# Reordering a decoder step: the stream's modulation slices, two places in ScalarE's list, four columns of the first stage, and unread identity products in TensorE's waits

## What is computed

```python
h = rms_norm(x, norm_mix_g) * (1 + scale1) + shift1        # modulation: silu(c) @ w_ada + b_ada, 6 x 1024 columns
q, k, v, qi, ki, wi, u, vg, g_a, g_b = split(h @ w_in)     # 512|128|128|256|64|4|512|512|1024|1024 columns
attn = sparse_attention(q, k, v, top_k(index_scores(qi, wi, ki)))   # 128 of 512 keys; samples: 256 of 2049, paged
gm = u * (tril(W_s) @ vg + b)                              # per chunk of 128
x = x + gate1 * ((g_a * attn @ w_proj_attn + g_b * gm @ w_proj_gmlp) @ w_out)
t = rms_norm(x, norm_ffn_g) * (1 + scale2) + shift2
x = x + gate2 * moe(t)                                     # best group of 4, best 2 of its 8 experts, SwiGLU width 256
```

## Time and profile before

| | |
|---|---|
| runs (3), us | median 780.42, 780.20 to 781.78 |
| the profiled execution's own time, us | 779.16 |
| its span, first to last instruction, us | 777.3 |
| TensorE busy | 733.2 us, 94% |
| VectorE busy | 409.5 us, 53% |
| ScalarE busy | 206.3 us, 27% |
| GpSimd busy | 169.5 us, 22% |
| mean granted TensorE clock, share of full | 0.988 |

### The profile page before, as it was taken

How to read it: one execution, slowest core, us unless ns; L and a number is a source line. 1 busy time by engine, 2 the same in 40 slices (tenths; PEclk the granted TensorE clock), 3 DMA queues, 4 the chain that set the end, 5 groups by cost and what they waited for, 6 DMA issues and landing times.

```text
span 777.3 us, 11077 instructions
## 1 busy us (share of the span) xinstructions
PE 733.2 (94%) x4211; PEld 454.5 (58%) x4211; DVE 409.5 (53%) x940; ACT 206.3 (27%) x418; POOL 169.5 (22%) x193
## 2 busy tenths in 40 slices
PE   5899999999999998999999999987999999999986
PEld 3444466588765565788788544555555555555442
DVE  4123299999989989820245324883532322322226
ACT  4113233414366767201200011221111111111112
POOL 2030012041000000055310002464233333333210
PEclk9999999999999999999999999997999999999999
DMA  8963032433056345553423752348999999999988
GB/s 343 407 214 104 1 108 76 185 140 119 9 197 236 133 191 218 190 174 102 152 56 150 273 220 108 110 171 349 418 428 423 427 425 426 422 426 422 425 345 329
DMA packets 29191, 187.60 MB, mean 241 GB/s; under 512 B 7194, under 2 KB 8158, under 8 KB 17742
## 3 DMA queue, kind: packets, MB, share of 16 engines
q1 hardware_dynamic: 18686, 164.86, 52.8%
q0 software_dynamic: 9536, 19.72, 7.7%
q10 hardware_dynamic: 912, 2.26, 0.8%
HBM read 180.77 MB, written 16.13 MB: 253 GB/s over the span
## 4 chain that ended last, share of the span: by engine, by line
PE 77%; DMA 11%; ACT 4%; DVE 4%; issue 2%; POOL 1%; SPq 0%; DVEq 0%; POOLq 0%; ACTq 0%
PE psum L784 22%; PE psum L1267 14%; PE psum L751 11%; PE psum L1281 7%; DMA arena<-in_experts 5%; PE psum L713 4%; PE psum L659 3%; PE psum L1260 2%; DMA ring<-in_stream 2%; ACT arena L1747 2%; PE psum L1168 1%; PE psum L971 1%; DMA arena<-in_cache_ki,stat 1%; PE psum L642 1%; PE psum L982 1%
## 5 line engine op out<-in xcount | busy, mean ns | idle before, releaser
L784 PE MATMUL psum<-hT,ring 128*128 128x260 f32 x640 | 143.2, 384 | 0.1
L784 PEld LDWEIGHTS psum<-hT,ring 128*128 128x128 f32 x640 | 120.7, 190 | 21.8 <-issue 3.3
L1747 ACT ACTIVATE arena<-psum 128x512 f32<-128x512 f32 (+11 forms) x127 | 68.5, 575 | 229.8 <-PE psum L784 70.4
L751 PE MATMUL psum<-ring,hT 128*128 128x512 f32 (+1 forms) x256 | 94.6, 523 | 0.0
L751 PEld LDWEIGHTS psum<-ring,hT 128*128 128x128 f32 x256 | 48.0, 192 | 42.8 <-issue 33.7
L1267 PE MATMUL psum<-ring,arena 128*64 128x256 f32 x608 | 70.6, 386 | 1.9 <-DMA ring<-in_experts 1.2
L1281 PE MATMUL psum<-arena 128*64 128x512 f32 x280 | 67.8, 605 | 0.8 <-issue 0.8
L1679 POOL DMA_INDIRECT expert_rows<-arena,router x34 | 34.4, 1013 | 140.2 <-DVE arena L2744 127.9
L1267 PEld LDWEIGHTS psum<-ring,arena 128*64 128x64 f32 x608 | 44.5, 140 | 32.2 <-issue 11.4
L2737 DVE COPY arena<-psum 128x128 f32<-128x128 f32 x35 | 10.2, 292 | 96.0 <-PE psum L1274 95.9
L784 PE MATMUL psum<-arena,ring 128*128 128x260 f32 x256 | 58.9, 386 | 0.0
(11 more groups left out here) (396 smaller groups left out, 945.7 us busy)
## 6 DMA issues: line engine op xcount, KB each, us to landing
ring<-in_stream SPq DMA_DIRECT2D x21, 2048.0 KB, 8.8
ring<-in_experts SPq DMA_DIRECT2D x16, 2048.0 KB, 18.7
arena<-in_experts SPq DMA_DIRECT2D x32, 1024.0 KB, 22.4
arena<-in_experts SPq DMA_DIRECT2D x11, 2048.0 KB, 23.3
hT<-in_experts SPq DMA_DIRECT2D x5, 2048.0 KB, 21.0
ring<-expert_rows SPq DMA_DIRECT2D x8, 512.0 KB, 7.4
ring<-in_stream SPq DMA_DIRECT2D x2, 1280.0 KB, 6.2
arena<-in_x_prompt SPq DMA_DIRECT2D x4, 512.0 KB, 5.7
```

Source lines behind the costliest of these rows:

```text
L751: mm = pe.matmul(psum[:, b, 0:width], hT[:, k, t * P:(t + 1) * P], w[:, k, :], start=(k == 0), stop=(k == KD - 1))
L784: mm = pe.matmul(psum[:, b0 + s, 0:HALF], w[:, k, f * P:(f + 1) * P], rhs[:, k, s * HALF:(s + 1) * HALF], start=(first and k == 0), stop=( ...
L1747: ins = act.activation(out, in_, func, scale=scale)
```

## The change

Five edits. (1) In the stream, G1 comes after ada5 and ada6 instead of before them, and ada5 takes slot 2 instead of slot 1. (2) In attention, ScalarE does the next group's exponentials before it copies the finished attention block out. (3) In routing, ScalarE's `x2T_out(1)` stands before `exponents(0)` and `square(2)`, no longer behind them. (4) The last `ada_columns(3)` stands inside `a_half(3, 0)`, after its second of four blocks. (5) A new `keep_busy(name, b, n)` puts n products of the identity matrix with itself into a bank that nothing reads; it is called at nine places (`idle0` to `idle8`) ahead of a wait.

```diff
-          + [(name, KD * 512) for name in ("G0", "ada4", "G1", "ada5", "ada6", "ada7", "ada8", "ada9", "ada10", "G2",
+          + [(name, KD * 512) for name in ("G0", "ada4", "ada5", "ada6", "G1", "ada7", "ada8", "ada9", "ada10", "G2",
                                            "G3", "ada11")]
-SLOTS = (0, 2, 1, BESIDE, 0, 2, 0, 1, 2) + (0, 1, 2, 1, 1, 0, 1, 0, 1, 0, 2, 1) + (1, 0, 2, 1)
+SLOTS = (0, 2, 1, BESIDE, 0, 2, 0, 1, 2) + (0, 1, 2, 1, 2, 0, 1, 0, 1, 0, 2, 1) + (1, 0, 2, 1)
...
-            def a_half(t, h):
+            def a_half(t, h, after={}):
...
+                    if k in after:
+                        after[k]()
...
+            def keep_busy(name, b, n):
+
+                banks.begin(pe, name, b)
+                for i in range(n):
+                    mm = pe.matmul(psum[:, b, 0:P], ident, ident, start=True, stop=True)
+                    if i == 0:
+                        banks.filled(mm, name)
+                banks.drained(mm, name)
+
             pe.wait_ge(const_in, 16)
+            keep_busy("idle0", 3, 16)
             x_transposes_of(0)
...
             x_transposes_of(1)
+            keep_busy("idle8", 3, 3)
             x_transposes_of(2)
+            keep_busy("idle1", 3, 3)
             x_transposes_of(3)
...
             ada_product(2, 1)
+            keep_busy("idle2", 0, 2)
             ada_columns(2)
+            keep_busy("idle3", 0, 4)
             ring_wait(pe, "A")
...
-            a_half(3, 0)
-            ada_columns(3)
+            a_half(3, 0, {1: lambda: ada_columns(3)})
...
                 banks.filled(mm, ("qkiT", t))
+                if t == 1:
+                    keep_busy("idle4", 2, 3)
...
                          "counts")
+            keep_busy("idle5", 4, 3)
             pick_sums(4)
+            keep_busy("idle6", 4, 2)
...
             gate_sums(4)
+            keep_busy("idle7", 6, 7)
...
                     evac(("probsT", g, c), [(probsT[:, c, :], psum[:, 4 + c % 2, :])])
+                if g + 1 < N_GROUPS:
+                    exponentials(g + 1)
                 if jp == 1:
                     evac(("att", qb), [(attT[:, :, qb * P:(qb + 1) * P],
                                         psum[:, 6 + qb % 2, :].rearrange("p (j n) -> p j n", j=4))])
-                if g + 1 < N_GROUPS:
-                    exponentials(g + 1)
...
             t2_store(0)
+            x2T_out(1)
             exponents(0)
             square(2)
-            x2T_out(1)
             t2_store(1)
```

## The result

| kernel | median us | lowest to highest | executions |
|---|---|---|---|
| before | 781.1 | 780.2 to 784.2 | 4 |
| changed | 772.04 | 770.36 to 775.75 | 4 |

The medians differ by 9.1 us, against 10.5 predicted. The ratio is 0.9889, with a 95% interval of 0.9856 to 0.9922. It is an estimate of its own, and here and in the experiments it differs by up to 0.002 from the quotient of the two medians, so a difference of 1 to 2 us between ratios says nothing. The profiled execution took 770.36 us with a span of 768.6 (before 777.3) and a mean clock of 0.993.

A forecast was written before the change was run, and what follows sets the result against it. TensorE's chain was taken to bound the time before the first gather, the weights' stream the expert stage after. Terms 0.9+1.4+1.0+1.4+2.4+2.6+1.0-0.2 = 10.5 us give 769.9 from 780.42; own range 767.5 to 772, 8-in-10 766.5 to 774.5.

The forecast's parts named there:

- rival B: Attention: VectorE sets the pace, ScalarE's reordering gives 1.0 and the DMA waits' 2.4 comes by half; 772.7 us, chance 0.12.
- The stream, 2.4: Attention: TensorE's DMA waits for ada5 and ada6, 1.12 and 1.28 us, go; 2.4 us gained.
- ScalarE in attention, 2.6: Attention: exponentials first remove 0.6 of TensorE's 1.04 us wait and all of the 2.04; 2.6 us gained.
- Routing, 1.0: Routing: TensorE's 1.66 us wait for ScalarE's copy goes, VectorE is late next, so 1.0 us goes on.
- Rival C: Routing gives nothing because VectorE and GpSimd fall into another pattern; 770.9 us, chance 0.1.
- `idle6`, -0.2: Ahead of `tables`: its products exceed the 0.51 us wait and `tables` writes the same bank; 0.2 us lost.
- `ada_columns(3)`, 1.0: First stage: moved columns let VectorE start modulating sooner, removing TensorE's 1.01 us wait before 48.87; 1.0 us gained.
- The clock: 0.9 + 1.4 + 1.4: First stage: identity products give 0.9 us at the start and prevent falls near 28 and 76 us, 1.4 each.
- Rival A: First stage: the clock falls all the same at 28 or 76 us, or first products stay slow; 773.6, chance 0.2.
- What bounds the expert stage: Expert stage: the weights' stream bounds it, its amount fixed from 531.51 us, so the end moves with that point.
- The late clock, 0: First expert block: a held clock makes products 1.6 us faster, but the weights' stream hides it; 0 gained.
- Rivals D and E: Expert stage: new interleaving slows the weights' stream (slower, 0.03); or its start is fixed by something else (780.4, 0.03).

The follow-up runs named there:

- routing_only: Kernel before with only ScalarE's `x2T_out(1)` moved ahead of `exponents(0)` in routing: 782.09 us, ratio 1.001.
- stream_act: Kernel before with the stream's new order and ScalarE's exponentials ahead of the attention block's copy, together: 777.4 us, ratio 0.9929.
- no_late_idle: Changed kernel without `idle5`, `idle6` and `idle7`: 774.31 us, ratio 0.9884.
- idle_only: Kernel before with the nine `keep_busy` calls and nothing else of the change: 781.59 us, ratio 0.9982.
- idle_transposes: Changed kernel with each identity product replaced by two transposes of the identity: 772.64 us, ratio 0.9868.
- half_down: Changed kernel loading only the first half of each down matrix for 26 late-stream experts: 767.35 us, ratio 0.9812.
- no_start_idle: Changed kernel without `idle0`, `idle8` and `idle1`: 772.19 us, ratio 0.9863.
- group 1: The first four experiments (no_idle, idle_only, stream_only, act_only), run on one chip beside the kernel before, which took 783.74 us there.
- stream_only: Kernel before with only the new order and slots of the stream: 782.35 us, ratio 0.9977.
- act_only: Kernel before with only ScalarE's exponentials ahead of the attention block's copy: 778.79 us, ratio 0.9931.
- changed again: The changed kernel, unedited, measured a second time beside the kernel before: 773.49 us, ratio 0.9898.
- no_idle: Changed kernel without any of the nine `keep_busy` calls, its four reorderings kept: 774.84 us, ratio 0.9889.

## Why the prediction was right, and where it was not

The time, 772.04, lies in the 8-in-10 range (766.5 to 774.5), 2.1 us above the point and at the very edge of the forecast's own range (to 772), near rival B's 772.7. The mechanisms of attention and routing were right. The clock's terms were right in size and wrong in that they were expected each time. The first stage gives 2.35 us in the mean over the traces, for 4.7 predicted, and this shortfall is as large as the whole miss. Term by term:

- **The stream, 2.4.** Both DMA waits went, 2.55 us at their place in every kernel with the edit. But its net worth in attention is 1.44: alone it loses 1.11, 0.98 of waits for VectorE among it, and the loss is not an accident of that run, since the pair gives 4.79 where the two alone would give 5.91. This is the half of rival B that came true.
- **ScalarE in attention, 2.6.** 3.35 for itself, 2.2 behind the stream's edit, because 0.34 of the 1.04 is then left, and VectorE holds TensorE up by 0.32 at 248.40. The prediction had this remainder (0.4), but charged it to the ScalarE edit alone. Sum of both terms: 5.0 predicted, 4.79 measured, 4.77 in the changed kernel.
- **Routing, 1.0.** 1.17 to 1.22 in that stretch in nine of nine traces. Rival C fell there; the median of routing_only does not show the gain.
- **`idle6`, -0.2.** 0.3 at full clock, about 0.5 at half.
- **`ada_columns(3)`, 1.0.** 1.17: the second column is 26.30 with the identity products and 25.13 with the edit beside them, both without a fall in it; it is 26.31 in stream_act, with neither and without a fall in it.
- **Price of an identity product, 0.27 and 0.49.** Four took 1.14 in the changed kernel at full clock, 2.05 in no_late_idle at half: 0.28 and 0.51. The 16 of `idle0` took 5.54 for an estimated 6.
- **The clock: 0.9 + 1.4 + 1.4.** These sizes are right when they come. A fall at 28 costs 1.71, one at 76 1.6. In the changed kernel's profiled execution none came, and the stage gave 4.66 for 4.7 predicted. That match was luck. The step that failed is "the fall at 28 should not come", and with it the 0.9 of `idle0`. With these products in the code the clock fell between 20 and 35 us in four of six traces (idle_only, idle_transposes, no_late_idle, half_down), 3.4 to 13.7 us long. The fall began ahead of the first tile, on the ada products and the identity products themselves, and the first "A" tile started at 28.0 to 31.0 in place of the 27.1 of before. Falls that early are not the products' own doing: stream_act, with none, had one at 16 to 20 us, and no_start_idle one at 17 to 21. Over all traces, a fall came before 35 us in six of six without `idle2` and `idle3`, and in five of eight with them.
- **The start's products.** Among the kernels that share the moved columns, `idle2`, `idle3` and `idle4`, the way to the first "U" averages 157.1 us over five traces with the start's products (154.76, 155.10, 156.24, 158.17, 161.08) and 155.7 over two without (155.07, 156.34). Rival A had the mechanism ("the first products stay slow", the clock falls all the same) and too small a chance. It is not one case beside the forecast but a draw at each execution. The draws, 154.8 to 161.1 us, are wide enough for the changed kernel's spread of 5.4 us, but they are not shown to be its cause: kernels without the moved columns and the products took 159.4 to 159.6 to that point in five of five, and yet the kernel before spreads from 781.3 to 789.7 us in group 1. What decides a draw stays open.
- **What bounds the expert stage** was right, by less than I thought. "From there the amount to transfer is fixed; the end moves with 531.51" fits before against changed (222.2 for 221.8 us). Blocks run at TensorE's 6.17 us each, and the stream shows only in the last three or four waits; but it sets the end, 3.4 us behind what TensorE alone would need (half_down). In the second execution of the changed kernel the first down product stood at 534.49, 2.3 us ahead of the other's 536.83; at the last one 0.25 was left (749.81, 750.06), and a fourth wait for weights, 1.39 us at 718.48 (first row at the end of this list), had taken most of it. A gain of TensorE's is lost there, as the prediction said.
- **The late clock, 0.** A loss of TensorE's is not always free. In stream_only the clock was down for 17 us in all from 525 on, and the DMA share in its window (second row there) fell to 0.91 from before's 1.00: the likely reason is that the loads, which wait for TensorE to free a buffer, came late. The stretch was 2.5 us longer. act_only (0.92 in a like window, 224.27) and idle_transposes (0.92, 223.87) are alike, and no other kernel with all its weights and a full stream is above 223.4 but stream_act, whose clock fell at 740 us, at the last blocks. "Late clock: 0" is therefore right only as long as the stream stays full. The 1.1 to 1.5 us more of no_start_idle have no such hole (0.99) and stay open.
- **A sign of being wrong** that the prediction named, the stretch from the gather to the end growing, came weakly: 246.7 us for 245.8. The same code gave 245.6 in its second execution, so the growth is not shown to be the change's. The other sign, a new wait at `gate_block(4)`, came too: 0.29 us at 234.95. It is not for G1's weights, which the prediction feared, but for VectorE, like the 0.32 at 248.40.

```profile
718.48 3.67 PE L1286 MATMUL psum<-hT,arena 128*64 128x256 f32 x32 [1.39 <-DMA hT<-in_experts]
...
541.00:561.00 20.00, 18.67 (x143) 11.54 (x144) 11.29 (x49) 2.55 (x5) 3.26 (x4) 0.91 0.91 366
```

The sum with these figures, for a mean over the traces: 2.35 for the first stage (159.42 - 157.07), 4.77, 1.2 and -0.3 give 8.0, less up to 1 us of spread in the gather, the expert stage and the tail. The medians say 9.1 in one measurement and 8.2 in another. The identity products' net share of it is not distinguishable from nothing: with all of them the ratios are 0.9889 and 0.9898, with none 0.9889, without the first three 0.9863, without the last three 0.9884, and all these intervals overlap. Alone they give 0.9982 [0.996, 1.0004], at most 3.1 us, where the prediction had 0.9 + 1.4 + 1.4 - 0.2 = 3.5 for them. As far as the medians can tell, the gain of the change is that of its four orders.

Rivals D and E fell: the DMA share from 561 to 741 us is 1.01 both before and after, and the end came 8.7 us earlier.

## What to carry to other kernels

Ask of a removed wait which engine is ready next to be late, and price the edits of one engine chain together: here the order on one queue was worth 1.1 us less than its waits, because VectorE was just behind. Work that only holds TensorE's clock is a bet: here the clock fell all the same in five of eight traces, and where it is down the added work itself costs nearly double. Size it by its slow price, so that it does not outlast the wait that it fills, and time such an edit over many executions; one profiled execution would have credited it with 3.5 us (4.66 less 1.17). To learn by how much a transfer bounds a stage, transfer less: what is left is the next bound, here 3.4 us below.

## What the runs showed of the hardware

The granted clock is not a function of the code. With the same first stage the clock held its full level from the first tiles to 514 us and beyond in two executions (changed, and changed again) and fell to half for 3.4 and 13.7 us in two others (half_down, no_late_idle); the wait for one 2 MB transfer beside it was 0.30 to 1.84 us, and the fall in half_down came with the wait of only 0.30, while 0.52 and 0.63 brought none, so the wait alone does not decide it. The same transfer, issued at the same time, took 15.7 us once and 17.1 once.

Thirty-two transposes of 128 columns brought TensorE from the slow to the fast price (0.14 us each in the tile that follows, before 0.24). In three kernels without them sixteen of the tiles' own did. The clock record shows the full level there too (1.00 in stream_only from 9 to 14 us, where eight transposes took 1.94), so at the start the durations are to be read and not the record.

TensorE stood idle 0.51, 0.87, 1.02 and 1.64 us in sum near 350 us in 4 of 14 executions (act_only, no_idle, idle_only, stream_only) without anything in the trace that it waited for. These four are the traces of group 1, all from one chip, and none of the other ten has it. The cause was not tried.
